# Stationary weights of two neighbouring input blocks stored alternately, in a float32 transformer block on one core

## What is computed

```
def _swiglu(h, w_gate, w_up, w_down):
    return (jax.nn.silu(h @ w_gate) * (h @ w_up)) @ w_down

yl, _, _ = _mixer(hl @ w_in[l], ...)      # 2048 -> 13,376 columns, and w_ssd_out, w_pool, w_fourier, w_out
x = x + g_m * yl
x = x + g_f * _swiglu(_rmsnorm(x, norm_ffn_w[l]) * (1 + sc_f) + sh_f,
                      w_ffn_gate[l], w_ffn_up[l], w_ffn_down[l])
```

## Time and profile before

| | us |
|---|---|
| three executions | 3446.16, 3475.79, 3482.48 |
| median | 3475.79 |
| span of the profiled execution (first to last instruction) | 3444.4 |
| PE busy | 3309.3, 96% of the span |
| PEld busy | 3069.0, 89% |
| DVE busy | 2384.8, 69% |
| ACT busy | 1559.9, 45% |
| DMA, mean over the span | 213 GB/s |

### The profile page before, as it was taken

The page is one execution under the profiler, slowest core; times in us unless marked ns, Lnnn a source line. Parts: engine busy times, 40 slices in busy tenths (PEclk is TensorE's granted clock), DMA queues, the critical chain, the costliest instruction groups (busy, mean ns, idle before and its releaser), DMA issues. The chain is left out here.

```text
span 3444.4 us, 58440 instructions
## 1 busy us (share of the span) xinstructions
PE 3309.3 (96%) x24696; PEld 3069.0 (89%) x24696; DVE 2384.8 (69%) x3425; ACT 1559.9 (45%) x2193; POOL 196.8 (6%) x364
## 2 busy tenths in 40 slices
PE   6989999999999989999999999999989899999999
PEld 3477788789999889999999989889978899999999
DVE  6776666547777777788788666776677677555554
ACT  2343545544434344443444554555455544444443
POOL 0000000000111000000001100010000000000000
PEclk8999999999999999999999999999999999999999
DMA  7732223548888768888878656565544588665566
GB/s 278 260 104 86 80 98 111 181 151 286 290 292 291 255 235 279 283 278 284 272 270 274 206 166 209 189 202 196 193 153 159 182 278 278 198 197 194 193 192 185
DMA packets 202437, 732.94 MB, mean 213 GB/s; under 512 B 23232, under 2 KB 23488, under 8 KB 201664
## 3 DMA queue, kind: packets, MB, share of 16 engines
q1 hardware_dynamic: 151632, 540.70, 46.4%
q0 software_dynamic: 49824, 183.52, 16.5%
q10 hardware_dynamic: 720, 4.98, 0.4%
HBM read 727.01 MB, written 2.10 MB: 212 GB/s over the span
## 5 line engine op out<-in xcount | busy, mean ns | idle before, releaser
L946 PE MATMUL ps<-hT,whi 128*128 128x256 f32 (+1 forms) x11360 | 2160.6, 292 | 0.0
L946 PEld LDWEIGHTS ps<-hT,whi 128*128 128x128 f32 x11360 | 1781.5, 189 | 58.1 <-issue 6.8
L946 PE MATMUL ps<-hT,wlo 128*128 128x256 f32 (+1 forms) x5680 | 1697.2, 299 | 55.3 <-DVE wlo L1869 18.7
L1869 DVE TENSOR_TENSOR wlo<-raw,whi 128x1024 fp32r<-128x1024 f32 (+1 forms) x978 | 1175.6, 1207 | 718.0 <-ACT whi L1436 715.7
L1436 ACT ACTIVATE whi<-raw 128x1024 fp32r<-128x1024 f32 (+1 forms) x978 | 1014.7, 1042 | 834.6 <-PE ps L946 821.2
L946 PEld LDWEIGHTS ps<-hT,wlo 128*128 128x128 f32 x5680 | 1081.2, 190 | 115.9 <-issue 74.9
L946 PE MATMUL ps<-t,whi 128*128 128x256 f32 x3136 | 539.9, 277 | 0.0
L946 PEld LDWEIGHTS ps<-t,whi 128*128 128x128 f32 x3136 | 475.0, 189 | 0.2
L946 PE MATMUL ps<-t,wlo 128*128 128x256 f32 x1568 | 437.0, 279 | 7.5 <-DVE wlo L1869 7.5
L946 PEld LDWEIGHTS ps<-t,wlo 128*128 128x128 f32 x1568 | 296.3, 189 | 8.9 <-DVE wlo L1869 8.7
L1884 DVE CUSTOM_DVE_ANT_0 t<-t,modv 128x1024 f32<-128x1024 f32 x192 | 243.2, 1280 | 9.1 <-DMA t<-in_w_mod 7.7
(11 more groups left out here) (233 smaller groups left out, 1742.0 us busy)
## 6 DMA issues: line engine op xcount, KB each, us to landing
raw<-in_w_in_s SPq DMA_DIRECT2D x250, 512.0 KB, 4.6
t<-in_w_mod POOLq DMA_DIRECT2D x192, 512.0 KB, 5.1
raw<-in_w_ffn_gu SPq DMA_DIRECT2D x176, 512.0 KB, 5.4
raw<-in_w_gu SPq DMA_DIRECT2D x176, 512.0 KB, 4.7
t<-in_w_ada_r POOLq DMA_DIRECT2D x128, 512.0 KB, 5.6
t<-in_w_ada_s SPq DMA_DIRECT2D x64, 512.0 KB, 4.5
raw<-in_w_out SPq DMA_DIRECT2D x64, 512.0 KB, 4.7
raw<-in_w_ffn_down SPq DMA_DIRECT2D x64, 512.0 KB, 4.6
```

Source lines behind the costliest of these rows:

```text
L946: return e.matmul(o, l, r, start=start, stop=stop)
L1869: tt(lo[:, 0:n], S.buf("raw", p)[:, 0:n], hi[:, 0:n].bitcast(F32), ALU.subtract).then_inc(*up("lo", p))
```

## The change

The host now stores two neighbouring blocks of 128 columns, `k` and `k+1` with `k` even, alternately: element 0 of block `k`, element 0 of block `k+1`, element 1 of block `k`, and so on, over 256 places. `kblock` addresses one of them with a step of two float32 elements (8 bytes): the even block from the pair's start, the odd one from one element further. The matmuls are otherwise the same, in the same number and order, with the same values. Weights that serve as moving operand (widths 512 and 256) are stored as before. On every engine the program has as many instructions as before, in the same order.

```diff
+    def kblock(w, k):
+
+        a = k // 2 * 2 * P + k % 2
+        return w[:, a:a + 2 * P - k % 2:2]
+
@@ product
-                c = slice(k * P, (k + 1) * P)
                 g.wait_ge(*inputs(t, i))
-                mm(ps, wlo[:, c], xhi, i == 0, False)
-                mm(ps, whi[:, c], xhi, False, False)
-                ins = mm(ps, whi[:, c], xlo, False, i == t.total - 1)
+                mm(ps, kblock(wlo, k), xhi, i == 0, False)
+                mm(ps, kblock(whi, k), xhi, False, False)
+                ins = mm(ps, kblock(whi, k), xlo, False, i == t.total - 1)
@@ pooled
-                c = slice((2 * i + k) * P, (2 * i + k + 1) * P)
+                c = 2 * i + k
                 xhi, xlo = dT[0][:, 2 * n + k, :], dT[1][:, 2 * n + k, :]
-                mm(ps, wlo[:, c], xhi, k == 0, False)
-                mm(ps, whi[:, c], xhi, False, False)
-                ins = mm(ps, whi[:, c], xlo, False, k == 1)
+                mm(ps, kblock(wlo, c), xhi, k == 0, False)
+                mm(ps, kblock(whi, c), xhi, False, False)
+                ins = mm(ps, kblock(whi, c), xlo, False, k == 1)
@@ blocks (host layout)
         b = w.reshape(split, k // P // split, P, c // width, width).transpose(3, 0, 2, 1, 4)
+        if width == P:
+            b = b.reshape(c // P, split, P, -1, 2, P).swapaxes(4, 5)
         b = np.ascontiguousarray(b).reshape(c // width, split, P, -1)
```

## The result

| | us |
|---|---|
| changed kernel, four executions | 3532.26 to 3537.33, median 3535.81 |
| kernel before beside it | 3446.16 to 3484.93, median 3479.14 |
| ratio of the times | 1.021, 95% interval 1.0145 to 1.028 |
| profiled execution of the changed kernel | 3537.21, span 3535.3 |

3395 us was forecast, with a range from 3360 to 3600 and 0.28 for slower. The time lies in the range and the direction was wrong. The changed kernel scatters by 5 us, the kernel before by 39 us.

A forecast was written before the change was run, and what follows sets the result against it. PE's matmul pitch was taken as the bound. From 3444 us, 43 us of stalls gone gave 3401, and 27 more with pitches at the load's floor gave 3374; 3395 us was forecast between them, range 3360 to 3600.

The forecast's parts named there:

- What bounds the kernel: PE's time between matmul starts, 113.3 or 117.7 ns at 256 columns; 1 ns is worth 20 us.
- nothing else would change: All engines: no instructions added, removed or moved; DMA, ACT and DVE handle the same bytes, at zero cost.
- the cost of the stepped read: Each weight load reading every second element: taken as zero extra, load durations staying at 189 ns.
- Rival 2: Stepped load needs somewhat more than 105 ns: about 3500 us at 117.5 ns, 3610 at 123; chance 0.20.
- The bounds from the rows: Stepped load's extra cost: zero if elements count, 11 ns if bytes count, 105 ns if half of each fetch is wasted.
- My 109 ns for the moving read: Estimate of what a float32r moving read of 256 columns needs alone, from plain float32 at 215 ns.
- the gain of 43 us: Reads at equal speed no longer meet: 34 us from slow 256-column matmuls, 9 us from 512-column ones.
- The prediction's own sign: In the new trace, a longer pitch at both 256 and 512 columns means the two reads hinder each other more.
- 512 columns: Matmuls with 512 moving columns: from 229.7 ns average to their best 225.4, 2,100 x 4.3 ns = 9 us gained.
- Rival 1: Nothing happens: both rhythms come from something in PE other than addresses and remain, 3440 to 3510 us; chance 0.27.
- Rival 3: The load doubles because fetched neighbouring elements are thrown away: 217 ns per 256-column matmul, about 5480 us; chance 0.08.
- an added 1.3 ns on the load: Load's floor of 112 ns lies 1.3 ns under the better pitch; any addition above that counts on every 256-column matmul.

The follow-up runs named there:

- The matmuls alone: Kernels running only the kernel's float32r matmuls from one SBUF region, no other engine working: at 256 columns 113.3 or 117.8 ns contiguous, 120.0 at step 2.
- The runs by the start: Matmuls alone, 256 moving columns, weights' start at 0 to 112 elements, moving operand at 80: step 1 113.3 to 120.0 ns, step 2 120.0 to 121.7.
- the best case of such a kernel: Matmuls alone with `wlo` at 0, `whi` at 32: 113.3 ns in all four streams; that edit in the kernel before: 3425.01 us against 3442.46, ratio 0.994.

## Why the prediction was wrong

**What bounds the kernel** was right: PE's pitch, two rhythms of it, 20 us for each ns, and no part of another engine. (Short slow stretches stand before 735.6 us too, from 213 us on; they hold some 500 matmuls and change nothing in it.) The matmuls alone reproduced 113.3 and 117.8 to a tenth of a ns. That nothing else would change was right too: instructions, ACT and DVE are as before.

**The step that failed is the cost of the stepped read, taken as zero.** The load alone goes from 111.7 to 117.8 ns, so the cost is 6 ns. In the kernel, where the load meets a moving read of 256 columns, the mean pitch of the stepped matmuls rose by 5 ns (115.0 to 120.0), in part by the second step that failed, below. Rival 2 had it, with 117.5 for its middle case. The bounds from the rows held (0 and 11 ns, with the doubling as far end). My reason for taking the lower one was that the moving read passes 1024 bytes in 113 ns as a matter of course. It does, but it takes all of 113.3 ns for it, with next to nothing to load beside it, and 229 ns once it has to pass 2048 bytes with a step of 8: the moving read is not a read with room to spare but one at its limit. A stepped load passes nearly the same 1024 bytes, and takes 117.8. My 109 ns for the moving read, an estimate from plain float32 at half the rate, hid that.

**The second step that failed is the picture behind the gain of 43 us.** The slow rhythm did disappear, and the scatter with it, as forecast; but what took its place was 120.0 ns, not 113.3. I had read two rhythms as two reads that meet now and then and would no longer meet at equal speed. The runs by the start show no start without stalls at step 2. (The sum was also too large for its own picture: some 700 of the 7,700 slow matmuls have their weights as the moving operand, which the change doesn't touch.) The interaction as such is real, though: at 256 columns neither read alone needs 120 ns (113.3 and 117.8), one stepped load of three gives it to the whole stream where the load times add up to 113.8, and contiguous loads reach it too from the start 16. So the load's own 6 ns would bring a stream to 117.8 at most, and only if every load is stepped; the rest up to 120.0 comes from the two reads holding each other up. Being near a bound is no condition for that, since 64 contiguous columns do it too (118.9). How much of the 4.7 ns is the one and how much the other is not shown, and what in the memory makes the reads hold each other up was not measured; only starts, steps and widths were. The prediction's own sign pointed there: a longer pitch at 256 and at 512 columns was to mean that the reads hinder each other more.

**512 columns** were expected to gain 4.3 ns and lost 2.9 (6 us in all; 384 of the 2,256 are untouched by the change). With a start of 0, the matmuls alone gave 228.9 or 233.3 at step 1 and 233.3 at step 2, the same pattern on a smaller scale.

**Rival 1** did not come: neither of the two rhythms is left where the kernel's loads are stepped. The same contiguous load makes the pitch 113.3 or 120.0 ns by its start alone, so addresses do count. The Trainium skill's page "TensorE: Matmul & The Clock Gate", section "Step-by-step: what each phase is for", says that a load takes no read bandwidth from the running matmul, each having a read port of its own; at this width these runs disagree. **Rival 3**, the doubling, needs step 4: a step of 2 costs a load 5%, steps 3 and 4 cost it 56% and 109%. The Trainium skill's page "Advanced Engine Details and Errata", section "SBUF Cachelines", asks for two hits to a line of 16 bytes for full speed. For the load that is nearly what was measured, and the 6 ns that are missing counted here, with the load within 2 ns of being the bound; for the moving operand it is not, since two hits to a line took 229 ns where four took 113.3.

**The size.** Against the profiled execution the forecast of rival 2's middle, 50 us, would have been too small (90.9), since it reckoned with 117.5 ns and not with 120.0. Of the sizes only the bounds of the load's cost held. The chance of 0.28 for slower was too low; that an added 1.3 ns on the load would count in full stood in the text, and should have weighed more than a gain that needed a picture no row showed.

## What to carry to other kernels

With a fresh weight load for every 256-column float32r matmul, load (111.7 ns) and moving read (113.3 ns) are balanced so closely that 6 ns more on the load, even on one load of three, made the pitch 120.0: keep stationary columns contiguous, and expect a step of 8 bytes to cost about 2% of such a kernel and one of 12 or 16 bytes to make the load the bound. Keep moving columns contiguous all the more: a step of 8 bytes doubled their read. With more moving columns the step in the weights cost between nothing (288, 320) and 4 ns (272, 384). Where the pitch has two values for one program, try the places of the operands within 256 bytes in a kernel of matmuls alone, the two halves of a split apart; here the best case of such a kernel carried over. Before a read is assumed to have room because another read goes at the same rate, measure both of them alone.

## What was not expected of the hardware

- The moving read of 256 float32r columns has a bound of its own of 113.3 ns, the same with 2 and 32 stationary columns and in the better rhythm of 128. With a load of 128 columns beside it the pitch is 123.3 ns at 272 columns, 133.4 at 288, 146.7 at 320 and 173.3 at 384. All of these are 1.77 to 1.85 ns for each place of 16 bytes that the moving read passes, and so are the 229 ns at a step of 8 bytes (1.79); that the price belongs to the place is an estimate from these figures.
- A load costs 1.82 ns for each place of 16 bytes once those decide (steps 3 and 4), and step 8 is only 3% dearer than step 4 (240.9 against 233.3 ns).
- The rhythm at start 32 alternated from stream to stream of the same form, whatever the width of the matmul between them. In the trace of the kernel before, all its changes but one came where a matmul was held up or one of another form lay between. That fits the scatter, up to 51 us in the kernel before and 2 to 8 us in the kernels with one rhythm; no trace of a slower execution was taken to show it.
- Offsets count to the single element: with `wlo` and `whi` one element apart, 117.7 to 120.0 ns.
